# Decoder trunk on 8 cores: where RMSNorm squares are summed, the order of the first pass, the conv taps, and the last output tile

## Chip, cores, metric

The kernel runs on all 8 cores of one Trainium2 chip. Every core runs the same program on its own 2048 tokens (plus 144 tokens to the left and 16 meta tokens) and nothing is exchanged. The metric is the device time in microseconds (us) of the slowest core. Lower is better.

## What is computed

Four pre-norm residual layers over one stream h of 1024 channels, then a final RMSNorm. The mixers of layers 0 to 3 are attention, short convolution, pooling, attention; every layer ends with a SwiGLU FFN of width 2816.

```
def rms_norm(x, g):
    y = xf * lax.rsqrt(jnp.mean(xf * xf, axis=-1, keepdims=True) + RMS_EPS)
    return (y * g).astype(x.dtype)
# layer i
    a = rms_norm(h, norm_mix[i])
    h = h + mixer(a)          # attention: window 128, 16 meta keys, sinks, relative bias
    h = h + swiglu(rms_norm(h, norm_ffn[i]), w_gate, w_up, w_down)
# short_conv_mixer
    gate_b, gate_c, u = jnp.split(h @ w_in, 3, axis=-1)
    z = gate_c * u
    conv = sum(conv_w[t] * zp[:, t:t + L] for t in range(3))
    return (gate_b * conv) @ w_out
```

## The kernel before, in words

Channels lie on partitions, in KC = 8 chunks of 128; tokens are the columns. A core's 2208 columns are cut into three passes (`PASS`), and each pass into two tiles: 416 and 256 columns in pass 0, 384 and 384 in passes 1 and 2. The residual h stays in SBUF in f32. Weights stream through a ring of 6 slots of 512 KB (`load_unit`, on POOL's queue, converted to bf16 by the DMA). A group is 8 (or 7) matmuls of 128x128 weights against one tile, accumulated in one of eight PSUM banks (`group`).

Everything is written out as one static order. `_run(main, side, share)` walks the steps of `main`, which are mostly groups of matmuls with a cost each, and drops the steps of `side` between them in proportion. An engine executes its instructions in just that order; all engines wait only on semaphores that `Prog.op` derives from reads and writes. `merge` interleaves lists evenly.

**The norm.** `norm_steps` (line 394) has two ways to sum the squares of the 8 chunks. With `quads=False` (`square`) ACT writes each square in bf16 into one of 4 buffers `sq`, and PE sums over partitions and chunks with 8 matmuls against `onesb`, three steps behind. With `quads=True` (`square4`) ACT writes the squares in f32 into one of 3 buffers `sqf`, DVE adds them in two sets of four (3 adds each; the last writes bf16 to `sq`), and PE needs 2 matmuls. Then `root` takes ln and exp on ACT, and `scale` writes the 8 normed chunks on DVE.

**Attention.** `attn_in` projects queries, keys and values; ACT evicts q and k, DVE evicts v. `attn_core` works on items (a block of 64 queries and one of two pairs `pr` of key heads; pair 0 needs only query chunks 0 to 3). An item is: 4 score matmuls, two `exp` of 128x512 in place in PSUM on ACT, two multiplications with the bias table on DVE (to `Pt`), 8 matmuls for values and denominators, ln and exp of the denominator on ACT (`rden`), and one multiplication back on DVE. Items advance in half steps: item i's scores are issued, and a full step later its value matmuls.

**Stages.** `ffn(i)` runs the FFN of step i (i = 3 * layer + pass) with the mixer of step i+1 and the norm of step i+2 beside it. Where step i+1 is attention (i = 0, 1, 8, 9, 10) its items and the norm steps go beside the FFN's matmuls (`beside`), and these norms have `quads=False`. The lines at the end of `build` (1273 to 1294) are the first pass, before any FFN: tile 0's norm, then `first` (q, k, v of tile 0, with the exponentials of the bias tables on ACT, `tables`, at its end), `second` (tile 1's q, k, v, with the first items beside it), the queries of pass 1, and the output projection of pass 0's attention. PE has three banks for groups there (`MAIN3`).

**Convolution.** A step of `conv_in` (line 1033) runs three groups (B, C, u) for one chunk and tile. ACT copies u from PSUM to `sgt`; DVE forms z = C*u in `zt`, scales it by tap 0 into `cacc`, adds taps 1 and 2, and multiplies by B into `qt`. There is one `zt` and one `cacc`; banks 0 to 2 rotate for B, banks 3 to 5 for C and u. ACT carries the last two columns of z in `zcar`.

**The end.** In `ffn(11)` the last third of the down projection is done tile by tile (384, then 384). The final norm of the first tile runs beside the second tile's groups, that of the second tile after them; each normed quarter of a tile is stored as soon as it is there.

## Time and profile before

| | |
|---|---|
| time of 3 runs | 2802.86 to 2804.58 us, median 2804.21 |
| the profiled execution | 2803.19 us |
| its span, slowest core (5) | 2801.7 us (the others 2799.1 to 2801.1) |
| mean granted TensorE clock, by core | 0.988 to 0.991 |
| busy: PE, DVE, ACT | 97%, 57%, 40% of the span |
| chain that ended last | 90% PE, 4% DVE, 2% DMA, 2% ACT |

The span is the time from the first to the last instruction of one core; the execution's own time is 1.5 us above it. A busy PE is not PE at its peak: a matmul's end is modelled, and waits shorter than its pipeline don't show. PE's pace is better read from how many matmuls start in a stretch. The granted clock is given as a share of 2.4 GHz. Nearly all operations carry line 126, the line of `Prog.emit` that issues them, so groups are told apart by their tiles: `sb_abf<-sb_h` is a norm's scaling, `ps<-sb_sq,sb_onesb` the matmul that sums squares, `sb_h<-ps,sb_h` the addition to the residual.

### The profile page before, as it was taken

To read this page: it belongs to the slowest core of one execution; us is meant where nothing else is said; L and a number is where in the kernel's file an instruction comes from. 1 tells how busy PE (TensorE), PEld (TensorE's weight loads), DVE (VectorE), ACT (ScalarE), POOL (GpSimd) and SP (SyncE) were. 2 spreads that over 40 slices of the span, in tenths; PEclk is the share of its full clock that TensorE was granted. 3 is DMA by queue.
4 is the path that set the end of the run, shared out by engine and by line. 5 is a ranking of instruction groups with operands and counts; after the bars stand their busy time and mean duration, and the time that the engine had idled before them with its cause. 6 is when DMAs were issued, how large, how long until landed. Compare 5 with 4: busy or idle time off the path is not lost.

```text
span 2801.7 us, 53884 instructions; the slowest of 8 cores (2799.1 to 2801.7 us)
## 1 busy us (share of the span) xinstructions
PE 2711.6 (97%) x18214; PEld 1674.1 (60%) x18214; DVE 1584.9 (57%) x3182; ACT 1126.1 (40%) x2370; POOL 280.3 (10%) x532
## 2 busy tenths in 40 slices
...
GB/s 235 57 71 94 95 98 93 89 83 105 89 104 101 106 107 120 106 98 102 92 110 102 91 122 108 116 100 113 90 88 108 109 121 109 88 91 107 104 117 117
DMA packets 82974, 290.93 MB, mean 104 GB/s; under 512 B 9940, under 2 KB 11924, under 8 KB 81940
## 3 DMA queue, kind: packets, MB, share of 16 engines
...
q8 instruction: 155, 2.54, 0.4%
q14 instruction: 111, 0.91, 0.1%
...
## 4 chain that ended last, share of the span: by engine, by line
PE 90%; DVE 4%; DMA 2%; ACT 2%; issue 2%; DVEq 0%; ACTq 0%; SPq 0%; POOL 0%; POOLq 0%
PE ps L126 90%; DMA sb_h<-x 1%; ACT sb_sgt L126 1%; DVE sb_Pt L126 1%; DMA sb_ring<-attn_q 1%; DVE sb_scr L126 1%; DVE sb_abf L126 1%; DVE sb_qt L126 0%; DVE sb_abm L126 0%; ACT ps L126 0%; DVE sb_sgt L126 0%; DVE sb_sqf L126 0%; DVE sb_h L126 0%; DVE sb_gbf L126 0%; ACT sb_rden L126 0%
## 5 line engine op out<-in xcount | busy, mean ns | idle before, releaser
L126 PE MATMUL ps<-sb_abf,sb_ring 128*128 128x384 bf16 (+2 forms) x8608 | 1369.7, 318 | 15.6 <-DVE sb_qt L126 5.2
L126 PEld LDWEIGHTS ps<-sb_abf,sb_ring 128*128 128x128 bf16 x8608 | 834.9, 98 | 512.0 <-issue 53.7
L126 PE MATMUL ps<-sb_gbf,sb_ring 128*128 128x384 bf16 (+2 forms) x4352 | 699.0, 317 | 2.9 <-DVE sb_gbf L126 2.1
L126 PEld LDWEIGHTS ps<-sb_gbf,sb_ring 128*128 128x128 bf16 x4352 | 417.8, 98 | 253.3 <-issue 25.2
L126 ACT ACTIVATE sb_sgt<-ps 128x384 f32<-128x384 f32 (+2 forms) x528 | 247.5, 469 | 732.1 <-PE ps L126 642.0
L126 DVE TENSOR_TENSOR sb_gbf<-ps,sb_sgt 128x384 bf16<-128x384 f32 (+2 forms) x528 | 281.7, 533 | 457.8 <-PE ps L126 372.4
L126 DVE TENSOR_TENSOR sb_h<-ps,sb_h 128x384 f32<-128x384 f32 (+2 forms) x624 | 329.9, 533 | 241.5 <-PE ps L126 237.3
L126 PE MATMUL ps<-sb_abm,sb_ring 128*128 128x384 bf16 (+2 forms) x1952 | 316.9, 323 | 7.0 <-DVE sb_scr L126 2.9
L126 PEld LDWEIGHTS ps<-sb_abm,sb_ring 128*128 128x128 bf16 x1952 | 191.7, 99 | 127.4 <-issue 21.5
L126 POOL DMA_DIRECT2D sb_ring<-ffn_gu x264 | 140.7, 533 | 1225.1 <-PE ps L126 1224.5
L126 ACT ACTIVATE sb_sqf<-sb_h 128x384 f32<-128x384 f32 (+2 forms) x256 | 120.9, 498 | 276.2 <-DVE sb_sqf L126 196.9
L126 DVE TENSOR_TENSOR sb_sgt<-ps,sb_sgt 128x384 f32<-128x384 f32 (+2 forms) x206 | 106.6, 517 | 207.6 <-ACT sb_sgt L126 194.9
L126 PE MATMUL ps<-sb_qt,sb_ring 128*128 128x384 bf16 (+3 forms) x1136 | 180.2, 316 | 0.0
L126 ACT ACTIVATE ps<-ps 128x512 f32<-128x512 f32 (+2 forms) x270 | 141.9, 563 | 86.6 <-PE ps L126 86.6
L126 DVE TENSOR_TENSOR sb_Pt<-ps,sb_eb 128x512 bf16<-128x512 f32 (+3 forms) x272 | 167.0, 652 | 12.9 <-ACT ps L126 11.3
L126 PEld LDWEIGHTS ps<-sb_qt,sb_ring 128*128 128x128 bf16 x1136 | 110.6, 98 | 62.9
L126 POOL DMA_DIRECT2D sb_ring<-ffn_dn x144 | 76.0, 527 | 680.3 <-PE ps L126 680.0
L126 ACT ACTIVATE sb_sgt<-sb_sgt,sb_oneb 128x384 f32<-128x384 f32 (+2 forms) x206 | 120.2, 584 | 19.6 <-ACT sb_sgt L126 0.7
L126 DVE SCALAR_TENSOR_TENSOR sb_abf<-sb_h,sb_gam,sb_rstd 128x384 bf16<-128x384 f32 (+2 forms) x208 | 113.1, 584 | 19.0 <-ACT sb_rstd L126 18.9
L126 ACT ACTIVATE sb_sgt<-sb_sgt 128x384 f32<-128x384 f32 (+2 forms) x206 | 101.3, 492 | 20.0 <-ACT sb_sgt L126 1.5
L126 ACT ACTIVATE sb_sq<-sb_h 128x384 bf16<-128x384 f32 (+2 forms) x176 | 82.1, 495 | 52.8 <-PE ps L126 34.8
L126 PE MATMUL ps<-sb_sq,sb_onesb 128*128 128x384 bf16 (+2 forms) x242 | 68.3, 321 | 33.0 <-DVE sb_sq L126 30.3
...
## 6 DMA issues: line engine op xcount, KB each, us to landing
sb_ring<-ffn_gu POOLq DMA_DIRECT2D x264, 512.0 KB, 6.5
...
sb_ring<-ffn_dn POOLq DMA_DIRECT2D x48, 512.0 KB, 6.3
sb_ring<-conv_in POOLq DMA_DIRECT2D x36, 512.0 KB, 6.4
sb_ring<-attn_q POOLq DMA_DIRECT2D x24, 512.0 KB, 7.1
sb_ring<-attn_o POOLq DMA_DIRECT2D x24, 512.0 KB, 6.4
...
sb_ring<-conv_out POOLq DMA_DIRECT2D x12, 512.0 KB, 6.2
```

The lines of the kernel that those rows point to most:

```text
L126: ins = getattr(e, name)(*a_, **kw_)
```

## The change

- **Sum of squares.** `quads` becomes 0, 4 or 8. With 8, DVE adds all eight chunks (7 adds) and PE does 1 matmul. It is used for the norms that run beside attention (`mixer_prep` and `final` in `ffn(0)`, `ffn(1)`, `ffn(8)`, `ffn(9)`, `ffn(10)`; 8 matmuls per tile before) and for the FFN norm beside the convolution of pass 0 in layer 1 (also 8 before). Pass 0's first norm goes from 4 (6 adds, 2 matmuls) to 0 (8 matmuls).
- **First pass.** Tile 0's q chunks 4 to 7 move behind its k and v (`more`), the items of pair 0 on tile 0's blocks come first, and all 23 items become one list that is cut over four stretches. PSUM: three banks for scores and one for outputs, for two and two. The loads that follow x's first tile on SP's queue wait until that tile has landed.
- **Convolution.** Tap 0 is applied by ACT into `sgt`, z has two buffers, and taps 1 and 2 with the product by B are issued one step later, behind the next step's z.
- **End.** Pass 2's last third of the down projection and its final norm use tiles of 384, 256 and 128 columns.

```diff
-OUT_TILES = tuple(n for _, n in LAST_TILES0) + tuple(n for p in PASS[1:] for _, n in p["tiles"])
+END_TILES = ((0, 384), (384, 256), (640, 128))
+OUT_TILES = tuple(n for t in (LAST_TILES0, PASS[1]["tiles"], END_TILES) for _, n in t)
...
-    zt = scr[:, 0:420]
-    cacc = scr[:, 420:836]
+    zts = [scr[:, 420 * i:420 * i + 420] for i in range(2)]
...
-    small += sload(attb[:], ab_d.rearrange("l p c -> p l c"), "s1", ("attb",))
+    P.op("sp", _I.dma_start(out=attb[:], in_=ab_d.rearrange("l p c -> p l c")), reads=[B("h", k, 0) for k in range(KC)],
+         writes=[B("attb")], dma="s1")
+    small.append(B("attb"))
...
-            if 0 <= j < KC and j % 4:
+            if 0 <= j < KC and j % quads:
                 f = st["f"][j]
-                acc = st["f"][j - 1] if j % 4 == 1 else st["acc"]
-                if j % 4 == 3:
+                acc = st["f"][j - 1] if j % quads == 1 else st["acc"]
+                if j % quads == quads - 1:
                     si = ctr["sq"] % NSQ
                     ctr["sq"] += 1
-                    st["sq"][j // 4] = si
+                    st["sq"][int(j == 7)] = si
                     out, key = sq[:, si, 0:n], B("sq", si)
                 else:
                     out, key = sqf[:, f, 0:n], B("sqf", f)
                     st["acc"] = f
                 P.op("dve", _I.tensor_tensor(out=out, in0=sqf[:, acc, 0:n], in1=sqf[:, f, 0:n], op=ALU.add),
                      reads=[B("sqf", acc), B("sqf", f)], writes=[key])
-            if k in (7, 11):
-                total(st["sq"][k // 8], k == 7, k == 11)
+            if (k == 7 and quads == 4) or k == 11:
+                total(st["sq"][k // 8], k == 7 or quads == 8, k == 11)
...
-        tiles = out_tiles(l, p)
+        tiles = END_TILES if last else out_tiles(l, p)
...
                 part = [(8 * t[1], lambda c=c, t=t: qstep(c, t)) for c in range(KC)]
+                if ti == 0:
+                    part, more = part[0:4], part[4:]
...
+                parts.append(part)
                 if ti == 0:
                     part.append((0, tables))
-                parts.append(part)
+                    parts.append(more)
...
-            items.append(("m", 0, 0, NMETA))
-            items += [(-3, pr, 16, 16) for pr in range(2)]
+
+            for pr in range(2):
+                items += [("m", 0, 0, NMETA)][0:pr] + [(-3, pr, 16, 16)] + [(jb, pr, _hbcol(p, jb), 64) for jb in range(-2, 4)]
         j0, j1 = PASS[p]["hb"]
-        if p == 0 and l > 0:
-            j0 = 0
+        if p == 0:
+            j0 = 0 if l > 0 else 4
...
-            P.op("act", _I.copy(out=sgt[:, si, 0:n], in_=ps[bU][:, 0:n]), reads=[psb[bU]], writes=[B("sgt", si)])
-            P.op("act", _I.copy(out=zt[:, 0:2], in_=zcar[:, c, :]), reads=[B("zcar", c)], writes=[B("zt2")])
-            P.op("dve", _I.tensor_tensor(out=zt[:, 2:2 + n], in0=ps[bC][:, 0:n], in1=sgt[:, si, 0:n], op=ALU.mult),
-                 reads=[psb[bC], B("sgt", si)], writes=[B("zt")])
-            P.op("act", _I.copy(out=zcar[:, c, :], in_=zt[:, n:n + 2]), reads=[B("zt")], writes=[B("zcar", c)])
-            P.op("dve", _I.tensor_scalar_mul(out=cacc[:, 0:n], in0=zt[:, 0:n], scalar1=cw[:, c:c + 1]),
-                 reads=[B("zt"), B("zt2"), B("cw")], writes=[B("cacc")])
-            for tap in (1, 2):
-                P.op("dve", _I.scalar_tensor_tensor(out=cacc[:, 0:n], in0=zt[:, tap:tap + n],
-                                                    scalar=cw[:, tap * KC + c:tap * KC + c + 1], in1=cacc[:, 0:n],
-                                                    op0=ALU.mult, op1=ALU.add),
-                     reads=[B("zt"), B("zt2"), B("cw"), B("cacc")], writes=[B("cacc")])
-            P.op("dve", _I.tensor_tensor(out=qt[:, c, t[0]:t[0] + n], in0=ps[bB][:, 0:n], in1=cacc[:, 0:n], op=ALU.mult),
-                 reads=[psb[bB], B("cacc")], writes=tk("qt", c, t[0], t[0] + n))
+            z, zk, z2 = zts[ti], B("zt", ti), B("z2", ti)
+            S = sgt[:, si, 0:n]
+            P.op("act", _I.copy(out=S, in_=ps[bU][:, 0:n]), reads=[psb[bU]], writes=[B("sgt", si)])
+            P.op("act", _I.copy(out=z[:, 0:2], in_=zcar[:, c, :]), reads=[B("zcar", c)], writes=[z2])
+            P.op("dve", _I.tensor_tensor(out=z[:, 2:2 + n], in0=ps[bC][:, 0:n], in1=S, op=ALU.mult),
+                 reads=[psb[bC], B("sgt", si)], writes=[zk])
+            P.op("act", _I.copy(out=zcar[:, c, :], in_=z[:, n:n + 2]), reads=[zk], writes=[B("zcar", c)])
+            P.op("act", _I.activation(out=S, in_=z[:, 0:n], func=AF.Identity, scale=cw[:, c:c + 1]),
+                 reads=[zk, z2, B("cw")], writes=[B("sgt", si)])
+
+            def taps():
+                for tap in (1, 2):
+                    P.op("dve", _I.scalar_tensor_tensor(out=S, in0=z[:, tap:tap + n], scalar=cw[:, tap * KC + c:tap * KC + c + 1], in1=S,
+                                                        op0=ALU.mult, op1=ALU.add),
+                         reads=[zk, z2, B("cw"), B("sgt", si)], writes=[B("sgt", si)])
+                P.op("dve", _I.tensor_tensor(out=qt[:, c, t[0]:t[0] + n], in0=ps[bB][:, 0:n], in1=S, op=ALU.mult),
+                     reads=[psb[bB], B("sgt", si)], writes=tk("qt", c, t[0], t[0] + n))
+            if late[0]:
+                late[0]()
+            late[0] = taps
+            if c == KC - 1 and ti == len(PASS[p]["tiles"]) - 1:
+                late[0] = None
+                taps()
...
-        prep = mixer_prep(i + 2, not has_core(i + 1))
+        prep = mixer_prep(i + 2, 8 if has_core(i + 1) else 4)
         if l == NLAYER - 1 and p > 0:
-            prep = final(p - 1, ((0, 0), (0, 1))[p - 1], not has_core(i + 1))
+            prep = final(p - 1, ((0, 0), (0, 1))[p - 1], 8 if has_core(i + 1) else 4)
...
-                (s0, e0), (s1, e1) = norm_ffn(*lp(i + 1), quads=lp(i + 2)[0] != 1)
+                (s0, e0), (s1, e1) = norm_ffn(*lp(i + 1), quads=8 if lp(i + 2)[0] == 1 else 4)
...
-            end = final(2, (0, 1), quads=False)
+            end = final(2, (0, 1, 2), quads=0)
             _run(dn[2][0:KC])
-            _run(dn[2][KC:], end[0])
-            for step in end[1]:
+            _run(dn[2][KC:2 * KC], end[0][0:NSTAT + 1])
+            _run(dn[2][2 * KC:], merge(end[0][NSTAT + 1:], end[1]))
+            for step in end[2]:
...
-    prep, prep1 = mixer_prep(0), mixer_prep(1)
+    prep, prep1 = mixer_prep(0, 0), mixer_prep(1)
     for step in prep[0]:
         step()
     load_late((2, 3), tk("abf", 7, 0, 32))
-    first, second = attn_in(0, 0, 0)
+    first, more, second = attn_in(0, 0, 0)
     queries, keys = attn_in(0, 0, 1)
     _run(first, prep[2] + prep[1], 0.9)
+    main_banks[0], s_banks[0], o_banks[0], n_banks[0] = MAIN3, (3, 4, 5), (6,), (7, 7)
+    core = attn_core(0, 0, attn_items(0, 0))
+    _run(more + second, merge(core[0:17], prep1[0]))
     load_late((4, 5), tk("gbf", 7, 0, 32))
-    items = attn_items(0, 0)
-    main_banks[0], s_banks[0], o_banks[0], n_banks[0] = MAIN3, (3, 4), (5, 6), (7, 7)
-    core0, core1 = attn_core(0, 0, items[0:15]), attn_core(0, 0, items[15:])
-    _run(second, core0[0:10] + prep1[0])
     P.alias([B("xl"), B("abl"), B("ebm")], tall("qt"))
-    _run(queries[0:KC + 1], core0[10:16] + prep1[1])
-    _run(queries[KC + 1:], core0[16:])
+    _run(queries[0:KC + 1], merge(core[17:28], prep1[1]))
+    _run(queries[KC + 1:], core[28:39])
     out0 = mixer_out(0)
-    _run(out0[0:KC], core1)
+    _run(out0[0:KC], core[39:])
```

How it moves instructions, at three places. On PE in the first pass, around tile 1's q groups (`sb_abf` 128x256), before:

```order
L126 MATMUL ps<-sb_Pt,sb_ones 64x256 x4
L126 MATMUL ps<-sb_abf,sb_ring 128x256 x24
L126 MATMUL ps<-sb_sq,sb_onesb 128x384
L126 MATMUL ps<-sb_abf,sb_ring 128x256 x8
L126 MATMUL ps<-sb_sq,sb_onesb 128x384
L126 MATMUL ps<-sb_abf,sb_ring 128x256 x16
L126 MATMUL ps<-sb_ring,sb_abf 128x256 x16
L126 MATMUL ps<-sb_abm,sb_ring 128x384 x8
```

and in the change:

```order
L126 MATMUL ps<-sb_sq,sb_onesb 128x384
L126 MATMUL ps<-sb_abf,sb_ring 128x256 x8
L126 MATMUL ps<-sb_gbf,sb_kt 128x256 x4
L126 MATMUL ps<-sb_abf,sb_ring 128x256 x8
L126 MATMUL ps<-sb_Pt,sb_va 64x256 x2
L126 MATMUL ps<-sb_Pt,sb_vbo 64x256 x2
L126 MATMUL ps<-sb_Pt,sb_ones 64x256 x4
L126 MATMUL ps<-sb_abf,sb_ring 128x256 x8
L126 MATMUL ps<-sb_gbf,sb_kt 128x256 x4
```

Before, six of tile 1's groups have no attention between them; now an item's scores or values stand between nearly every two groups. On DVE at the start of pass 0's convolution in layer 1 (a step of 416 columns, then one of 256; `sb_abf` is the FFN norm beside it), before:

```order
L126 TENSOR_TENSOR sb_scr<-ps,sb_sgt 128x416
L126 TENSOR_SCALAR sb_scr<-sb_scr,sb_cw 128x416
L126 SCALAR_TENSOR_TENSOR sb_scr<-sb_scr,sb_cw 128x416 x2
L126 TENSOR_TENSOR sb_qt<-ps,sb_scr 128x416
L126 SCALAR_TENSOR_TENSOR sb_abf<-sb_h,sb_gam,sb_rstd 128x384 x2
L126 TENSOR_TENSOR sb_scr<-ps,sb_sgt 128x256
```

and in the change:

```order
L126 TENSOR_TENSOR sb_scr<-ps,sb_sgt 128x416
L126 SCALAR_TENSOR_TENSOR sb_abf<-sb_h,sb_gam,sb_rstd 128x384 x2
L126 TENSOR_TENSOR sb_scr<-ps,sb_sgt 128x256
L126 SCALAR_TENSOR_TENSOR sb_sgt<-sb_scr,sb_cw,sb_sgt 128x416 x2
L126 TENSOR_TENSOR sb_qt<-ps,sb_sgt 128x416
```

The z of the second step now stands ahead of the first step's taps, and the TENSOR_SCALAR is gone. On DVE at the very end, the last tiles' residual additions and scalings, before:

```order
L126 TENSOR_TENSOR sb_h<-ps,sb_h 128x384 x13
L126 SCALAR_TENSOR_TENSOR sb_abm<-sb_h,sb_gam,sb_rstd 128x384
L126 TENSOR_TENSOR sb_h<-ps,sb_h 128x384
L126 SCALAR_TENSOR_TENSOR sb_abm<-sb_h,sb_gam,sb_rstd 128x384 x3
L126 TENSOR_TENSOR sb_h<-ps,sb_h 128x384
L126 SCALAR_TENSOR_TENSOR sb_abm<-sb_h,sb_gam,sb_rstd 128x384 x2
L126 TENSOR_TENSOR sb_h<-ps,sb_h 128x384
L126 SCALAR_TENSOR_TENSOR sb_abm<-sb_h,sb_gam,sb_rstd 128x384 x2
L126 SCALAR_TENSOR_TENSOR sb_qt<-sb_h,sb_gam,sb_rstd 128x384 x8
```

and in the change:

```order
L126 TENSOR_TENSOR sb_h<-ps,sb_h 128x384 x8
L126 TENSOR_TENSOR sb_h<-ps,sb_h 128x256 x8
L126 TENSOR_TENSOR sb_h<-ps,sb_h 128x128 x8
L126 SCALAR_TENSOR_TENSOR sb_abm<-sb_h,sb_gam,sb_rstd 128x384 x5
L126 SCALAR_TENSOR_TENSOR sb_qt<-sb_h,sb_gam,sb_rstd 128x256
...
L126 SCALAR_TENSOR_TENSOR sb_qt<-sb_h,sb_gam,sb_rstd 128x256 x2
L126 SCALAR_TENSOR_TENSOR sb_qt<-sb_h,sb_gam,sb_rstd 128x128 x8
```

All scalings, those of the 384 tile too, now stand behind the last addition: the 128-column groups have a negative cost in `_run` (7 * 128 - 1300), so no side step is placed between them.

## Rows read from the trace of the kernel before

**Rows 1.** Page, head and part 1: span, busy time and share by engine.

```profile
span 2801.7 us, 53884 instructions; the slowest of 8 cores (2799.1 to 2801.7 us)
...
PE 2711.6 (97%) x18214; PEld 1674.1 (60%) x18214; DVE 1584.9 (57%) x3182; ACT 1126.1 (40%) x2370; POOL 280.3 (10%) x532
```

**Rows 2.** Stretches: PE, PEld, DVE, ACT, POOL busy (count), PEclk, DMA share, GB/s.

```profile
1240.00:1280.00 40.00, 40.00 (x248) 24.10 (x247) 15.05 (x28) 3.88 (x8) 3.70 (x7) 1.00 0.60 100
```

**Rows 3.** The same view, stretches of the first pass.

```profile
53.24:83.64 30.40, 21.05 (x153) 13.29 (x150) 15.83 (x42) 19.99 (x46) 2.64 (x5) 0.78 0.74 158
83.64:113.36 29.72, 21.97 (x113) 9.72 (x111) 18.46 (x37) 14.18 (x30) 0.53 (x1) 0.83 0.22 35
113.36:140.81 27.45, 23.33 (x149) 10.56 (x149) 16.15 (x34) 17.04 (x36) 1.58 (x3) 0.75 0.31 54
140.81:170.41 29.60, 22.89 (x163) 10.55 (x161) 17.69 (x32) 14.80 (x33) 0.53 (x1) 0.94 0.13 23
```

**Rows 4.** PE's waits from 53.24 to 170.41: us in total, times, longest.

```profile
PE ps L126 <- DVE sb_Pt L126: 14.5, 22, 2.0
PE ps L126 <- DVE sb_sq L126: 7.1, 3, 3.4
```

**Rows 5.** Timeline of POOL and ACT, start of the first pass: start us, us, instruction.

```profile
15.10 1.58 POOL L126 DMA_DIRECT2D sb_ring<-attn_q  x3 [12.88 <-DMA sb_h<-x]
49.78 3.60 ACT L126 ACTIVATE sb_eb<-sb_eb 128x4096 f32<-128x4096 f32 x1
58.71 0.41 ACT L126 ACTIVATE sb_qt<-sb_sinkst 1x256 f32<-1x256 f32 x1
```

**Rows 6.** Issues up to 62 us: KB each, median us to landing.

```profile
sb_ring<-attn_v POOLq DMA_DIRECT2D x1, 512.0 KB, 30.5
```

**Rows 7.** Timeline of PE in `ffn(1)` beside attention, two sums of squares.

```profile
642.53 0.49 PE L126 MATMUL ps<-sb_sq,sb_onesb 128*128 128x384 bf16 x2
642.86 1.46 PE L126 MATMUL ps<-sb_qt,sb_ring 128*128 128x384 bf16 x8
```

**Rows 8.** Groups by form, whole span: busy us, mean ns | idle before, releasers.

```profile
L126 DVE TENSOR_TENSOR sb_sqf<-sb_sqf 128x384 f32<-128x384 f32 x80 | 44.1, 552 | 21.2 <-ACT sb_sqf L126 18.7 <-DVE sb_sqf L126 2.2 <-ACT sb_gbf L126 0.2
...
L126 DVE TENSOR_TENSOR sb_sqf<-sb_sqf 128x256 f32<-128x256 f32 x28 | 11.8, 421 | 14.6 <-ACT sb_sqf L126 13.7 <-DVE sb_sqf L126 0.9
```

**Rows 9.** Stretches as in rows 2: FFN beside attention; conv of pass 0; after it.

```profile
2240.00:2280.00 40.00, 39.12 (x371) 30.39 (x371) 29.14 (x66) 32.18 (x76) 4.23 (x8) 1.00 0.69 113
...
650.33:715.63 65.30, 57.15 (x394) 37.84 (x392) 48.71 (x97) 16.52 (x58) 6.94 (x13) 0.99 0.68 111
715.63:721.10 5.47, 5.47 (x18) 2.54 (x19) 0.02 (x1) 1.77 (x2) 0.00 (x0) 0.50 0.27 50
```

**Rows 10.** PE's waits from 650 to 721 us.

```profile
PE ps L126 <- DVE sb_qt L126: 5.2, 1, 5.2
PE ps L126 <- DVE sb_scr L126: 2.9, 6, 0.8
```

**Rows 11.** Groups by form: the tap that leaves DVE.

```profile
L126 DVE TENSOR_SCALAR sb_scr<-sb_scr,sb_cw 128x384 f32<-128x384 f32 x32 | 13.4, 420 | 5.6 <-DVE sb_scr L126 5.6
```

**Rows 12.** The end: stretch (as rows 2), then DVE's timeline; last, 256-column scalings elsewhere.

```profile
2776.70:2801.70 25.00, 12.61 (x74) 6.98 (x72) 14.00 (x25) 9.00 (x17) 0.00 (x0) 0.83 0.33 127
...
2790.26 0.55 DVE L126 TENSOR_TENSOR sb_h<-ps,sb_h 128x384 f32<-128x384 f32 x1
2793.68 5.10 DVE L126 SCALAR_TENSOR_TENSOR sb_qt<-sb_h,sb_gam,sb_rstd 128x384 f32<-128x384 f32 x8 [1.61 <-ACT sb_rstd L126]
```

**Rows 13.** Small forms: PE's timeline near 45 us; DVE's scaling of 256 and of 144 columns.

```profile
44.88 0.66 PE L126 MATMUL ps<-sb_qt,sb_ring 128*128 128x144 bf16 x8
45.38 1.57 PE L126 MATMUL ps<-sb_abf,sb_ring 128*128 128x416 bf16 x8
...
52.25 0.88 DVE L126 SCALAR_TENSOR_TENSOR sb_abf<-sb_h,sb_gam,sb_rstd 128x256 bf16<-128x256 f32 x2
...
L126 DVE SCALAR_TENSOR_TENSOR sb_qt<-sb_qt,sb_gam,sb_rstd 128x144 bf16<-128x144 f32 x8 | 2.9, 368 | 3.6 <-ACT sb_rstd L126 2.9
```

More of the change, by code:

```diff
@@ L459, in scale @@
             ri = st["ri"]
-            P.op("dve", _I.scalar_tensor_tensor(out=dst(k), in0=hsrc(k), scalar=g[:, k:k + 1], in1=rstd[:, ri, 0:n],
+            P.op(eng, _I.scalar_tensor_tensor(out=dst(k), in0=hsrc(k), scalar=g[:, k:k + 1], in1=rstd[:, ri, 0:n],
                                                 op0=ALU.mult, op1=ALU.mult),
@@ L486, in q_of, with norm_mix @@
         return (gbf, "gbf") if (l, p) == (0, 0) else (qt, "qt")
-    def norm_mix(l, p, quads=True):
+    def norm_mix(l, p, quads=4):
         parts = []
@@ L587, in ffn_gu, with ffn_dn @@
         return steps
-    def ffn_dn(l, p, g, tile_major=False):
+    def ffn_dn(l, p, g, last=False):
         steps = []
@@ L601, in ffn_dn @@
         order = [(m, ti) for m4 in (0, 4) for ti in range(len(tiles)) for m in range(m4, m4 + 4)]
-        if tile_major:
+        if last:
             order.sort(key=lambda x: x[1])
@@ L1038, in prelude @@
             if p == 0:
-                claim("scr", [B("zt"), B("zt2"), B("cacc")])
+                claim("scr", [B("zt", i) for i in range(2)] + [B("z2", i) for i in range(2)])
         def step(c, ti, t):
@@ L1142, in build, with final @@
     out_sems = []
-    def final(p, regions, quads=True):
+    def final(p, regions, quads=4):
         parts = []
-        for t, r in zip(out_tiles(NLAYER - 1, p), regions):
+        for t, r in zip(END_TILES if p == NPASS - 1 else out_tiles(NLAYER - 1, p), regions):
             src, keys = h_tile(p, t)
             n = t[1]
-            name = ("abm", "qt")[r]
+            name = ("abm", "qt", "qt")[r]
             quarter = [B("yf", r, i) for i in range(KC // 2)]
-            y = (abm_raw, qt_raw)[r][:, 0:2 * KC * n].bitcast(F32)
+            y0 = 2 * KC * 256 if r == 2 else 0
+            y = (abm_raw, qt_raw, qt_raw)[r][:, y0:y0 + 2 * KC * n].bitcast(F32)
             def begin(name=name, quarter=quarter):
@@ L1162, in store @@
                      reads=[quarter[i]], dma=sem)
-                if i == KC // 2 - 1:
+                if i == KC // 2 - 1 and p < NPASS - 1:
                     P.alias(quarter, tall(name))
             steps = norm_steps(src, keys, n, gcol("fin", 0), lambda k, y=y, n=n: y[:, k * n:(k + 1) * n],
-                               lambda k, quarter=quarter: [quarter[k // 2]], quads)[0]
+                               lambda k, quarter=quarter: [quarter[k // 2]], quads,
+                               "pool" if POOL_SCALE and p == NPASS - 1 and r == 0 else "dve")[0]
             ends = [[steps[NSTAT + 2 * i], steps[NSTAT + 1 + 2 * i], lambda i=i, store=store: store(i)] for i in range(KC // 2)]
@@ L1176, in lp, with mixer_prep @@
         return i // NPASS, i % NPASS
-    def mixer_prep(i, quads=True):
+    def mixer_prep(i, quads=4):
         if i >= N:
```

11 lines of the change are left out of this document (6 added, 5 removed).

## The prediction

> **What bounds the kernel now.** I read the page's head and busy shares first, then stretches of 40 us, then PE's waits, then timelines where a stretch falls short. PE is busy 97% of the span, DVE 57%, ACT 40% [rows 1]. A typical FFN stretch starts 248 matmuls of 384 columns in 40 us, one per 0.161 us at full clock [rows 2]: that is PE's pace, 0.42 ns per column. So from the first FFN to the last tile the time is the sum of PE's columns, and work on DVE or ACT there costs nothing while it is on time. Three places fall short. (1) The first pass: in 117 us from 53.24 to 170.41 PE's clock is 0.75 to 0.94, and PE waits 14.5 us for `Pt` and 7.1 us for sums of squares [rows 3, 4]. (2) The convolution of pass 0: PE waits 2.9 us in six gaps for z and 5.2 us in one at the end, and the clock stands at 0.50 for the next 5.5 us [rows 9, 10]. (3) The last 25 us, of which PE works 12.6 [rows 12].
>
> **Sums of squares.** In the steady part the change takes 7 of 8 `onesb` matmuls from each of 12 tiles: two in each of the steps 0, 1, 8, 9 and 10, and two in the FFN norm before the convolution. That is 56 matmuls of 384 columns, 7 of 416 and 21 of 256. Two of them take 0.33 us [rows 7], the pace of any other. By columns 56 x 0.161 + 7 x 0.175 + 21 x 0.108 = 12.5 us. PE is the bound there, so this is taken whole: **-12.5 us**.
>
> In exchange DVE gets 7 adds per tile, 84 in all, at 0.55 us (384), 0.42 (256) and about 0.58 (416) [rows 8]: 56 x 0.55 + 21 x 0.42 + 7 x 0.58 = 43.7 us. In the fullest stretch beside attention DVE is busy 29.1 and ACT 32.2 of 40 us [rows 9]. There are 12 steps in 2801.7 us, some 230 us each, so 14 adds (8 us) bring DVE's load up by some 4%. The adds go in one per side step. A square must now wait until the add two places back has read its buffer; that add sits behind at most a few DVE instructions, as in the norms that already sum this way, where DVE's adds wait for ACT 18.7 us over 80 adds rather than the other way for long [rows 8]. The softmax chain behind it on ACT is what PE would notice. I take **+1.5 us**, near nothing, because PE shows about a microsecond lost even in the fullest stretch (39.12 of 40) [rows 9]; the ends are 0 and +10 (a quarter of the adds open).
>
> **First pass.** From 53.24 to 170.41 at full pace PE would need: 128 matmuls of 384 (20.6 us), 96 or so of 256 (10.4), 64 of 416 (11.2), and 20 items of 12 matmuls of 256 (26), together 68 us of 117. ACT is busy 66.0 us and DVE 68.1 us in the same stretch (sums over rows 3). [rows 3] No engine is full, so what limits is the chain of an item (scores, exp, weigh, values) with too little between its links in some places and no item at all in others. By stage, needed over taken: 13.6 of 30.4 (0.45), 15.5 of 29.7 (0.52), 22 of 27.5 (0.80), 22 of 29.6 (0.74). The thin ones are those where q groups stand alone while the dense ones wait on `Pt` [rows 3, 4]. The change spreads the items at 5 to 6 per eight groups. If every stage reaches the 0.77 of the two dense ones, 68 us take 88; 32 matmuls of tile 0's q that move in add 5.6 / 0.77 = 7 us, and they leave a stretch that waits for ring loads, so their going gives nothing there. That is 95 for 117: -22. Against it: the table exponentials hold ACT from 49.8 to 59.1 [rows 5] and can't be spread, and with three banks PE gets past them by three groups only; +4. For it: k and v are the third and fourth ring loads, not the fifth and sixth; v lands at 17.2 + 30.5 = 47.7 us now [rows 6] and I expect the order to give 2 to 4 us, of which I count 1. The load of x's first tile has the DMA engines to itself and the next ring loads wait for it until 15.1 us [rows 5]; with bf16 squares and no add behind the last one, -2; the bias table then is issued some 11 us later, which eats 1. In sum **-20 us**.
>
> The ends: everything in time, PE at its own need of 74 us in the stretch, gives -43; the late table load or one output bank (a value matmul waits until the item before is multiplied back) could take all of it and 5 us more, +5. I take the middle because the estimate rests on two stages of this very trace.
>
> Of the 49 us lost in the stretch the clock is a part: 0.22 x 30.4 + 0.17 x 29.7 + 0.25 x 27.5 + 0.06 x 29.6 = 20.4 us of full pace not granted [rows 3], which is 41 us at 1.2 instead of 2.4 GHz. So an order that keeps the clock up and changes no gap at all would still give up to -20. The Trainium skill puts the price of the clock in the same way (TensorE: Matmul & The Clock Gate, section "HAM oscillation — how this bites in real kernels"): the extra wall time of a throttled stretch is its length times one minus the clock ratio. By that page the whole gain of the first pass could be clock, with the gaps as they are, where my sum by stages lays it to closed gaps; the trace agrees on the size with its 20.4.
>
> **Convolution.** Behind a z stood the taps of the step before and two scalings; now z is first, and 0.42 us per step goes to ACT [rows 11], which is busy only 16.5 of 65 us [rows 9]. DVE needs 48.7 of 65.3 us there now; it loses 6 and gains the second tile's adds. The six gaps (2.9 us) close. The last one stays: the FFN's first group needs the bank of the last B, which is read after two steps' taps; copy 0.4, z 0.4, taps and product 1.9 and 1.5, so about 4.4 for 5.2. The half clock behind it stays. **-3.5 us**; ends -8 (clock kept) and 0.
>
> **The end.** The second tile starts at 2776.7; its last addition ends at 2790.8, the last scaling at 2798.8, the span at 2801.7 [rows 12], 25.0 us after it. Changed: 56 matmuls of 256 (6.0), 8 sums (1.3) and 56 of 128 columns. 144-column matmuls start every 0.063 us [rows 13], so these take at most 3.5. The last addition is done 11.2 us after the start, 2.9 earlier. But all 24 scalings now come after it: 5.1 (384) [rows 12], 8 x 0.44 = 3.5 (256), 8 x 0.32 = 2.6 (128, below the 0.37 of 144 columns) [rows 13]. They end at 22.4, where they end now at 22.1, and the last store follows with 2.9: **0 us**. Ends: -3 (PE's sums of the small tiles hidden and cheaper scalings) and +2.
>
> The last store gets three times smaller. The Trainium skill (DMA: Bandwidth & Descriptors, "Anatomy of one DMA — SWDGE (gpsimd) path") puts a transfer at about 2.0 us plus its bytes over 436 GB/s. By that estimate 393 KB cost 2.9 us, which is what the trace shows behind the last scaling, and 131 KB cost 2.3: the end would be -0.6, not 0.
>
> **Sum.** 2803.2 - 12.5 + 1.5 - 20 - 3.5 + 0 = 2768.7, against the profiled execution; the median of the runs is 1 us above it. I say **2769**.
>
> **Rivals.**
> - *The first pass hardly moves.* The chain of an item, not the spacing, sets the pace: one output bank now, the same two exps and two weighs. For it: PE's longest single waits are on `Pt` [rows 4], and the dense stages are no better than 0.80. Against: two stages at 0.45 to 0.52. The first pass gives -20 to 0; 2779 to 2789, and with costly adds up to 2798.
> - *It closes whole.* With the gaps the half clock goes too; -38 instead of -20, about 2750. For it: each engine needs under 60% of the time. Against: the tables, the loads.
> - *The adds lie open (slower).* Each add delays a square, the square the exp behind it on ACT, the exp a score or value matmul at which PE stands. Price: all 43.7 us. Then 2768.7 + 42 = 2811. It decides from about 35 us on, four adds of five. Against: the fullest stretch has DVE idle 11 of 40 us, and each add has a whole side step to pass in.
> - *The clock stays down.* Evenly spread short waits could keep PE at 1.2 GHz through the first pass, where now it is granted 0.75 to 0.94: at 0.6 the 74 us take 123, so the stretch gains nothing, 2791.
>
> **How the numbers follow.** About 0.2% (5.6 us) is what a measurement of this kernel tells from no change. Forecast (2757 to 2779): 0.52. First pass hardly moves or clock down (2779 to 2798): 0.26. Closes whole (2740 to 2757): 0.14. Within 5.6 us of before: 0.04. Slower by more, by open adds: 0.04. Hence faster 0.92. The range 2748 to 2792 leaves out the tails of both neighbours, about 2 in 10.
>
> **What would show it.** Right: 64 fewer matmuls on `onesb`, the small last tile's included; the stretches beside attention start the same groups 12 us sooner in sum, with PE still at 39 to 40 of 40; the first FFN begins some 20 us earlier; in the convolution no PE wait on `sb_scr`, one of 4 to 5 us at its end, and half a clock after it; at the end 24 scalings in a row on DVE. Wrong: ACT waiting for `sb_sqf` by tens of us with PE waiting on `Pt` in the stretches from 200 to 600 and 2150 to 2500 us; the first pass's clock at 0.8 or lower with as many waits on `Pt`; the last 25 us longer or shorter by more than 3.

## The result and the profile after

The changed kernel takes 2772.55 and 2774.99 us; the ratio to the kernel before is 0.9893, with a 95% interval of 0.9869 to 0.9917: 30 us less (23 to 37). I had said 2769, range 2748 to 2792. Some executions run on the cores of a die at a lower granted clock and take longer (two of this kernel's four, 2837.6 and 3140.9 us); they are left out of what follows, as are such cores in *The first pass alone* and *Eight chunks in the other norms too*. The execution profiled below took 2772.55 us; its slowest core is core 0 (before: core 5). It has PE at 97%, DVE at 57% and ACT at 41% of the span, as in [rows 1]:

```profile
span 2771.0 us, 53987 instructions; the slowest of 8 cores (2767.8 to 2771.0 us)
...
PE 2689.8 (97%) x18206; PEld 1665.3 (60%) x18206; DVE 1590.7 (57%) x3222; ACT 1148.8 (41%) x2428; POOL 280.2 (10%) x532
```

To see where 30 us went I cut both traces at the same places in the program. The rows are stretches (PE, PEld, DVE, ACT, POOL busy, PEclk, DMA share, GB/s). First the kernel before: up to the first FFN; from it to the convolution of layer 1, pass 0; the middle, from some 44 us behind that convolution to the first FFN with layer 3's attention beside it; from there to the last FFN (attention late).

```profile
0.00:194.90 194.90, 136.84 (x867) 72.80 (x868) 111.19 (x233) 101.32 (x219) 11.42 (x25) 0.89 0.56 123
194.90:650.33 455.43, 454.83 (x3198) 271.81 (x3196) 273.59 (x527) 263.68 (x546) 43.64 (x82) 1.00 0.55 92
...
759.89:1946.52 1186.63, 1183.16 (x7622) 745.04 (x7620) 675.01 (x1382) 317.56 (x653) 131.89 (x250) 1.00 0.63 106
1946.52:2535.46 588.94, 581.51 (x4330) 368.72 (x4330) 358.74 (x730) 350.35 (x750) 59.50 (x111) 1.00 0.59 101
```

Then the same of the changed kernel, with its convolution (that of before is in [rows 9]) and the 44 us behind it:

```profile
0.00:174.44 174.44, 125.54 (x878) 68.92 (x879) 103.64 (x221) 99.32 (x219) 11.42 (x25) 0.92 0.63 137
174.44:625.81 451.37, 449.85 (x3164) 268.33 (x3162) 288.11 (x562) 263.89 (x546) 43.63 (x82) 1.00 0.57 93
625.81:689.93 64.12, 56.32 (x386) 36.85 (x385) 45.34 (x88) 23.60 (x75) 6.87 (x13) 0.98 0.69 111
689.93:733.86 43.93, 43.93 (x257) 25.83 (x257) 8.37 (x15) 9.56 (x19) 3.70 (x7) 0.95 0.55 93
733.86:1920.50 1186.64, 1183.17 (x7622) 744.96 (x7621) 658.04 (x1350) 334.01 (x685) 131.92 (x250) 1.00 0.65 105
1920.50:2505.02 584.52, 575.95 (x4288) 364.48 (x4288) 375.44 (x772) 350.28 (x750) 59.49 (x111) 1.00 0.61 101
```

The gain by stage: first pass 20.5, next stage 4.1, convolution 1.2 (65.30 to 64.12), the 44 us behind it 0.3, the middle nothing (1186.63 and 1186.64), attention late 4.4, and from there to the end 0.3 (266.24 to 265.98). That is 30.7, the difference of the spans is 30.7. Between the first FFN and the last tile the same code takes the same time to 0.1 us on every core, but for a stretch of low clock behind the convolution (43.3 to 44.3 us there), so these lengths tell apart what the interval of the runs, some 7 us each way, can't. The start and the end don't repeat so well. The first FFN begins between 192.4 and 195.1 us on the eight cores before (median 194.6), and between 171.6 and 174.4 now (median 173.1); from the last stage's start to the end of the span it is 266.0 to 266.3 us before and 266.0 to 266.6 now, so the 0.3 us there are nothing. Where single cores differ so, I compare the medians of all eight.

**The start** did not gain. The changed kernel, timelines of PE, ACT and SP's queue (start us, us, instruction, idle before it and what ended it):

```profile
18.77 7.13 PE L126 MATMUL ps<-sb_abf,sb_ring 128*128 128x416 bf16 x16 [2.37 <-DVE sb_abf L126]
36.76 0.28 PE L126 MATMUL ps<-sb_sq,sb_onesb 128*128 128x144 bf16 x1 [10.86 <-DVE sb_sq L126]
...
29.21 0.61 ACT L126 ACTIVATE sb_gbf<-ps,sb_attb 128x416 bf16<-128x416 f32 x1 [11.42 <-DMA sb_qt<-bias_mm]
34.63 0.75 ACT L126 ACTIVATE sb_sqf<-sb_qt 128x144 f32<-128x144 f32 x3 [4.81 <-DMA sb_qt<-x]
...
14.63 0.39 SPq L126 DMA_DIRECT2D sb_attb<-attn_b  x1
...
18.18 0.59 SPq L126 DMA_DIRECT2D sb_qt<-x  x1
```

The held bias table stands ahead of everything else in SP's queue, so the 144 columns of x on the left are issued at 18.18 instead of 8.08 us and land only when ACT starts on them at 34.63; their first sum stands in PE's order, and PE waits 10.9 us. In and behind that wait its clock is granted at half for about 14 us: 0.81 from 19.2 to 35.0 and 0.83 from 35.0 to 58.0, which is 0.38 x 15.8 + 0.34 x 23.0 us at 1.2 GHz (what of it lies inside the wait costs nothing). The v groups that ended at 53.24 end at 56.74 (medians 53.3 and 56.5).

**The rest of the first pass** more than made up for it. Stretches as in [rows 3], the last one up to the first FFN, then PE's waits from 56.74 to 149.70 as in [rows 4]:

```profile
56.74:86.80 30.06, 24.50 (x196) 13.98 (x193) 21.73 (x50) 26.22 (x57) 1.06 (x2) 0.89 0.46 127
86.80:130.70 43.90, 36.14 (x294) 18.63 (x290) 32.29 (x71) 32.07 (x75) 3.93 (x8) 1.00 0.57 101
130.70:149.70 19.00, 17.04 (x125) 8.57 (x124) 12.09 (x23) 10.23 (x23) 0.30 (x1) 1.00 0.20 38
149.70:174.44 24.74, 20.76 (x143) 14.78 (x142) 17.39 (x39) 9.68 (x21) 2.63 (x5) 0.86 0.69 107
...
PE ps L126 <- DVE sb_gbf L126: 7.0, 8, 2.8
PE ps L126 <- DVE sb_Pt L126: 5.9, 4, 3.5
```

The 117.2 us of [rows 3] have become 93.0 with 5.6 us more of work in them. The waits for `Pt` fell from 14.5 us in 22 places to 5.9 in 4. New are 7.0 us in 8 places for the multiplication back (`gbf`), which frees the one output bank; they were 0.9 us in one place before. The clock is granted whole from 86.8 to 149.7 on this core (core 2 has 0.97 there), and at 0.86 in the stretch behind, which takes 24.7 us for 24.5.

**The convolution of pass 0.** PE's waits in it; they answer to [rows 10]:

```profile
PE ps L126 <- DVE sb_qt L126: 7.6, 8, 4.9
PE ps L126 <- DVE sb_scr L126: 0.2, 1, 0.2
```

The waits for z are gone, 2.9 us to 0.2, and seven new ones, 2.7 us in all, stand beside the long one, which is 4.9. What they are for shows in the timelines of PE and DVE at one of them:

```profile
640.08 2.62 PE L126 MATMUL ps<-sb_abm,sb_ring 128*128 128x416 bf16 x14 [0.43 <-DVE sb_qt L126]
...
637.84 0.59 DVE L126 TENSOR_TENSOR sb_scr<-ps,sb_sgt 128x416 f32<-128x416 f32 x1 [0.98 <-ACT sb_scr L126]
638.35 1.06 DVE L126 SCALAR_TENSOR_TENSOR sb_sgt<-sb_scr,sb_cw,sb_sgt 128x256 f32<-128x256 f32 x2
639.51 0.42 DVE L126 TENSOR_TENSOR sb_qt<-ps,sb_sgt 128x256 bf16<-128x256 f32 x1
```

DVE makes z of this step (416 columns), then the taps and the product of the step before (256). PE's next group is the B of the step after next, and B has three banks in turn: it needs the one that this product reads. A step of 256 columns leaves it 2.6 us after the last U, and ACT's copy, z, two taps and a product take about that (0.51 + 0.59 + 1.06 + 0.42), so PE waits at the end of each of these.

**The end** came out as worked. DVE's last two rows and SP's last:

```profile
2757.54 3.12 DVE L126 SCALAR_TENSOR_TENSOR sb_abm<-sb_h,sb_gam,sb_rstd 128x384 f32<-128x384 f32 x5 [0.16 <-DVE sb_h L126]
...
2764.93 4.00 DVE L126 SCALAR_TENSOR_TENSOR sb_qt<-sb_h,sb_gam,sb_rstd 128x256 f32<-128x256 f32 x10
...
2766.06 3.27 SPq L126 DMA_DIRECT2D out<-sb_qt  x5
```

All 24 scalings follow the last addition without a gap, 2757.54 to 2768.93 us, 11.4 us; the span ends 2.1 us later, not 2.9. Counted from the second tile's first matmul, the last scaling ends at 22.7 us on all cores, where it ended at 22.0 before, and the span ends 2.1 to 2.7 us behind it, where it was 2.7 to 3.0: the later scalings and the shorter tail cancel.

### The profile page after: what moved, and what is told of

The parts are those of the page before. It is cut to its first block, busy times and chain, and to the rows that moved or that the text cites. A ratio compares the mean times of both kernels' runs of the same rounds, so it can differ in the third digit from the quotient of the medians.

```text
span 2771.0 us, 53987 instructions; the slowest of 8 cores (2767.8 to 2771.0 us)
## 1 busy us (share of the span) xinstructions
PE 2689.8 (97%) x18206; PEld 1665.3 (60%) x18206; DVE 1590.7 (57%) x3222; ACT 1148.8 (41%) x2428; POOL 280.2 (10%) x532
## 4 chain that ended last, share of the span: by engine, by line
PE 89%; DVE 4%; ACT 3%; issue 2%; DMA 1%; SPq 0%; DVEq 0%; ACTq 0%
PE ps L126 89%; ACT sb_sgt L126 2%; DVE sb_Pt L126 1%; DVE sb_qt L126 1%; DVE sb_sgt L126 1%; DMA sb_qt<-x 1%; DVE sb_scr L126 1%; ACT ps L126 0%; DMA sb_h<-x 0%; DVE sb_gbf L126 0%; DVE sb_abm L126 0%; DVE sb_sqf L126 0%; DVE sb_abf L126 0%; DVE sb_h L126 0%; ACT sb_sqf L126 0%
## 5 line engine op out<-in xcount | busy, mean ns | idle before, releaser
L126 PE MATMUL ps<-sb_abf,sb_ring 128*128 128x384 bf16 (+2 forms) x8608 | 1366.2, 318 | 11.4 <-DVE sb_qt L126 4.9
L126 DVE TENSOR_TENSOR sb_h<-ps,sb_h 128x384 f32<-128x384 f32 (+3 forms) x632 | 330.8, 527 | 229.5 <-PE ps L126 224.2
L126 PE MATMUL ps<-sb_abm,sb_ring 128*128 128x384 bf16 (+2 forms) x1952 | 308.7, 318 | 5.6 <-DVE sb_qt L126 2.7
L126 ACT ACTIVATE sb_sqf<-sb_h 128x384 f32<-128x384 f32 (+2 forms) x336 | 160.0, 496 | 292.6 <-DVE sb_sqf L126 209.0
L126 DVE TENSOR_TENSOR sb_sqf<-sb_sqf 128x384 f32<-128x384 f32 (+3 forms) x196 | 102.0, 520 | 46.1 <-ACT sb_sqf L126 41.9
L126 ACT ACTIVATE sb_sgt<-sb_sgt,sb_oneb 128x384 f32<-128x384 f32 (+2 forms) x206 | 120.2, 584 | 19.6 <-ACT sb_sgt L126 0.8
```

The costliest lines, as they stand in the source:

```text
L126: ins = getattr(e, name)(*a_, **kw_)
```

## The experiments

All run on all cores beside the kernel before; "alone" is on the kernel before, the others on the changed one.

**The sums alone.** The edit, with its three callers giving 8 beside attention and convolution:

```diff
-            if 0 <= j < KC and j % 4:
+            if 0 <= j < KC and j % quads:
...
-            if k in (7, 11):
-                total(st["sq"][k // 8], k == 7, k == 11)
+            if (k == 7 and quads == 4) or k == 11:
+                total(st["sq"][k // 8], k == 7 or quads == 8, k == 11)
```

> The kernel before with the sums over eight chunks alone. Theory (from the two traces): the 84 ones-matmuls gone are 12.2 us of PE's columns, and the added DVE adds give about 2 us of it back in short waits near attention, so about 2794 us (-10). Rival 1: the adds cost PE nothing and the missing gain lies in another part, 2791.5 (-12.3). Rival 2: the adds lie open, 2800 or more.

2797.1 us median, ratio 0.9979 (0.9967 to 0.9990), about -6. Three stages on core 5, as above: before the convolution, the convolution, attention late.

```profile
196.20:647.22 451.02, 449.81 (x3163) 268.37 (x3161) 288.04 (x561) 263.82 (x546) 43.64 (x82) 1.00 0.55 93
647.22:713.63 66.41, 56.33 (x387) 36.96 (x385) 52.26 (x104) 16.77 (x59) 7.09 (x13) 0.97 0.64 108
...
1943.60:2528.58 584.98, 576.15 (x4287) 364.39 (x4287) 376.10 (x772) 350.47 (x750) 59.52 (x111) 1.00 0.59 101
```

The two stages beside attention give 4.4 and 4.0 us. 77 of the 84 ones-matmuls lie there (49 of 384 columns, 7 of 416, 21 of 256), 11.4 us at 0.42 ns a column, so the adds cost 3.0 us of them. In the convolution it is 1.1 us longer with 1.1 us fewer columns: seven adds cost 2.2 us where DVE has 52.3 of 66.4 us to do. So the sums alone give some 7 us by stages, and beside the late taps, where the convolution gains its 1.2 us, some 8. The theory's -10 is not reached in either.

**The taps alone.**

```diff
-            P.op("dve", _I.tensor_scalar_mul(out=cacc[:, 0:n], in0=zt[:, 0:n], scalar1=cw[:, c:c + 1]),
+            P.op("act", _I.activation(out=S, in_=z[:, 0:n], func=AF.Identity, scale=cw[:, c:c + 1]),
...
+            if late[0]:
+                late[0]()
+            late[0] = taps
```

> The kernel before with the late taps alone. Theory: the six waits for z (2.9 us) are replaced by as many short waits for the B bank, whose product now comes a step later, so the convolution of pass 0 keeps its length: 2803 to 2804.5 us (0 to -1), with PE waiting some 2.5 us in short gaps on the product. Rival, my prediction: -3.5, 2800.5; then it is the second tile's adds that refill the gaps in the changed kernel.

Ratio 0.9996 (0.9985 to 1.0008). The convolution takes 63.87 us for 65.30; PE's waits in it:

```profile
PE ps L126 <- DVE sb_qt L126: 6.3, 4, 5.0
PE ps L126 <- ACT sb_sq L126: 0.2, 1, 0.2
```

Alone the late taps give 1.4 us: three short waits for the bank, 1.3 us, for six of 2.9. With the second tile's adds on DVE there are seven. So both halves of the question hold: the waits moved to the bank, and the adds made more of them. The run's ratio can't show 1.4 us; the stage does, at 63.8 to 63.9 us on all eight cores.

**The first pass alone.** The order of the items, the banks, bf16 squares and the hold, as in the change.

> The kernel before with the new first pass alone (bf16 squares, held bias table, early k and v, even items, three score banks and one output bank). Theory: all of the 20.5 us by which the first FFN starts earlier reaches the end: about 2783.5 us (-20.5), first FFN at 174 us. Rival: the pass gains only together with other parts, or the later passes give some of it back (x tiles 2 to 5 load later): 2786 to 2793.

There is no ratio for this run; cores 4 to 7 span 2778.7 to 2781.1 us, some 20 below before. On core 6:

```profile
0.00:171.83 171.83, 124.18 (x878) 68.31 (x879) 103.36 (x221) 99.48 (x219) 11.47 (x25) 0.94 0.64 139
171.83:627.28 455.45, 454.84 (x3198) 271.86 (x3196) 273.75 (x527) 264.01 (x546) 43.84 (x82) 1.00 0.55 92
```

The stage behind it keeps its 455.4 us: nothing is given back, the theory holds.

**The split last tile alone.**

```diff
+END_TILES = ((0, 384), (384, 256), (640, 128))
...
-            _run(dn[2][KC:], end[0])
+            _run(dn[2][KC:2 * KC], end[0][0:NSTAT + 1])
+            _run(dn[2][2 * KC:], merge(end[0][NSTAT + 1:], end[1]))
```

> The kernel before with the split last tile alone. Theory: the later start of the scalings cancels the earlier last addition, 2803.5 us (0 to -0.5). Rival: the smaller last store and the cheaper scalings show, -2 to -3, and in the whole change something else takes them back.

Ratio 1.0006 (0.9994 to 1.0018): no change, as expected.

**No hold.** The bias table and what stands behind it in SP's queue are issued at once:

```diff
-    P.op("sp", _I.dma_start(out=attb[:], in_=ab_d.rearrange("l p c -> p l c")), reads=[B("h", k, 0) for k in range(KC)],
-         writes=[B("attb")], dma="s1")
+    small += sload(attb[:], ab_d.rearrange("l p c -> p l c"), "s1", ("attb",))
```

> The changed kernel, its bias table, x_left and x tile 1 issued at once again (no hold behind x tile 0). Theory: the hold is a loss. In the changed trace the 16 first matmuls end at 25.9 us and PE then stands 10.9 us for the sums of x_left, which lands at 34.6 because it was issued at 18.2; ACT's drain waits for the bias table until 29.2. Without it x_left lands some 8 to 10 us sooner, the first FFN starts 4 to 7 us earlier (168 to 170 us), the time is 2766 to 2769. Rival (my prediction): x tile 0 alone on the DMA engines is a gain; without the hold the first q group starts 1 to 2 us later and the end too, 2774 to 2776.

2767.3 us, ratio 0.9865 (0.9844 to 0.9886). Timeline of PE:

```profile
18.84 7.22 PE L126 MATMUL ps<-sb_abf,sb_ring 128*128 128x416 bf16 x16 [2.37 <-DVE sb_abf L126]
26.05 0.28 PE L126 MATMUL ps<-sb_sq,sb_onesb 128*128 128x144 bf16 x1
30.33 2.93 PE L126 MATMUL ps<-sb_abf,sb_ring 128*128 128x416 bf16 x8 [4.00 <-DMA sb_ring<-attn_q]
```

The first q group starts at 18.84 here against 18.77 us on core 0 of the changed kernel, but that core is the latest of its eight. On core 4, with the hold and without:

```profile
18.01 2.19 PE L126 MATMUL ps<-sb_abf,sb_ring 128*128 128x416 bf16 x4 [2.37 <-DVE sb_abf L126]
...
18.91 1.07 PE L126 MATMUL ps<-sb_abf,sb_ring 128*128 128x416 bf16 x2 [2.37 <-DVE sb_abf L126]
```

By medians the first q group starts at 18.1 with the hold (17.8 to 18.8) and at 18.9 without (18.3 to 19.2): alone on the DMA engines x's first tile does land some 0.8 us sooner, as the rival has it. But without the hold the sum of x_left is there when PE comes to it, and 4.0 us of waiting for weights stand where 10.9 stood. The first FFN starts at 166.1 to 169.4 us, median 166.7 for 173.1: in sum the hold cost 6.4 us.

**The hold moved to x tile 1.** As above, with `reads=` of x tile 0 at `x_load(1, "x2")`.

> The changed kernel, the hold moved from the bias table to x tile 1 (1 MB), so that the small tables and x_left go at once and the large loads behind x tile 0. Theory: takes the gain of both, first FFN at 166 to 170 us, 2764 to 2768, not slower than without any hold. Rival: the second x tile, whose sums stand in PE's order at 48 to 52 us, lands later and gives part of it back: same as with the hold, 2772.

2768.3 and 2767.8 us, ratio 0.9867 (0.9846 to 0.9889); first FFN at 166.5 to 169.8, median 167.5. No better than no hold: holding the large loads has no use either, and the first q group starts at 18.9 as without any, so the 0.8 us above are given by holding what stands ahead of x tile 1.

**Two score and two output banks.**

```diff
-    main_banks[0], s_banks[0], o_banks[0], n_banks[0] = MAIN3, (3, 4, 5), (6,), (7, 7)
+    main_banks[0], s_banks[0], o_banks[0], n_banks[0] = MAIN3, (3, 4), (5, 6), (7, 7)
```

> The changed kernel with two score banks and two output banks in the first pass, as before, in place of three and one. Theory A: the even spacing of the items made the gain, and the first FFN starts within 3 us of the changed kernel's 174.4 us (2771 to 2776). Theory B: the third score bank made it, since an item's scores can be issued while the two exps of the item before still hold theirs: the first FFN starts at 180 to 190 us, 2778 to 2788.

2778.4 us, ratio 0.9905 (0.9890 to 0.9921); first FFN at 175.8 to 180.7 us, median 178.9. PE's longest group of waits in the pass:

```profile
PE ps L126 <- DVE sb_Pt L126: 9.8, 13, 3.7
```

The time is in theory B's range, the start of the first FFN between the two. The waits for `gbf`, 7.0 us with one output bank, are gone, and those for `Pt` are 9.8 in 13 places for 5.9 in 4. So some 6 of the 21 us are what a third score bank gives beyond what the second output bank did; the rest is left to the spacing and order of the items, which no run changed by themselves. The single output bank, in which I saw the danger, does make PE wait and is still the better trade.

**C, U, B.** A convolution step issues its groups in another order:

```diff
-            banks = []
-            for part in range(3):
+            banks = {}
+            for part in (1, 2, 0):
```

> The changed kernel with the three groups of a convolution step in the order C, U, B. Theory: the short waits in the convolution of pass 0 are for the B bank, which the late product of three steps before still holds when B is the first group of a step; as the last group it is asked for two groups later, so all seven or so (0.6 us each, some 3 us) go, and the last one falls from 5.1 to about 3.5 us: -3 to -5 from 625.8 to 733.9 us, 2768 to 2770. Rival: the wait is DVE's pace (it needs as long as PE in this stretch), and the gaps only move to another bank: 2772 to 2774.

2770.2 us, ratio 0.9873 (0.9856 to 0.9891). The stage, and PE's waits in it:

```profile
629.25:688.59 59.34, 55.22 (x387) 37.46 (x386) 45.34 (x88) 23.74 (x75) 6.86 (x13) 1.00 0.65 112
...
PE ps L126 <- DVE sb_qt L126: 3.9, 1, 3.9
PE ps L126 <- DVE sb_scr L126: 0.2, 1, 0.2
```

The seven short waits are gone with DVE as loaded as before (45.34 and 45.34 us): they were for the bank, not DVE's pace. The stage gives 4.8 us, and the other convolutions in the middle another 2.5 (1184.1 for 1186.6). The run shows less, since on its slowest core the first FFN happened to start at 177.9 and late attention took 586.3 us, as on three of the eight cores (584.8 on the others).

**C, U, B, and the FFN's banks turned by three.** Three more `nxt("main", main_banks[0])` at the end of this convolution, so that the FFN's first group doesn't ask for the last B's bank.

> The changed kernel with the convolution in the order C, U, B, and the rotation of FFN's banks moved on by three after the convolution of pass 0, so that the FFN's first groups take the banks of the last C and U and reach the last B's bank fourth, not first. Theory: the remaining wait of 3.9 us goes, 59.3 us become 55.5 to 56, and with it perhaps the 6.8 us of half clock behind it (another 2 to 3): 2762 to 2766. Rival: the wait is for something else (the FFN's input), and stays: 2768 to 2770 as with C, U, B alone.

2765.3 us, ratio 0.9862 (0.9845 to 0.9879).

```profile
627.16:683.00 55.84, 55.24 (x388) 37.47 (x386) 42.41 (x83) 23.14 (x74) 5.81 (x11) 1.00 0.65 114
683.00:724.59 41.59, 41.59 (x256) 25.04 (x257) 11.30 (x21) 10.18 (x21) 4.75 (x9) 1.00 0.69 116
724.59:1912.49 1187.90, 1183.69 (x7623) 744.83 (x7620) 658.47 (x1350) 334.28 (x685) 131.90 (x250) 1.00 0.64 105
...
PE ps L126 <- DVE sb_qt L126: 3.2, 4, 2.1
```

The long wait goes (3.5 us), and the half clock behind it (42.9 to 44.3 us become 41.6, at 1.00). But the turn shifts the banks of later passes too, and the middle takes 1187.9 us (up to 1189.3 on other cores), 3.8 to 5.2 more than with C, U, B alone. The last row shows where: in the middle PE waits four times, 3.2 us, for a product (`qt`), each time at the start of the FFN behind a later convolution; with C, U, B alone it waits there for none. The banks should be turned back after use, which was not tried.

**Each add of the eight-chunk sums twice.**

```diff
+                for _ in range(2 if quads == 8 else 1):
```

> The changed kernel with each add of the sums over eight chunks made twice, 588 - 504 = 84 more DVE adds of about 0.52 us (43.7 us of DVE); the repeated add counts a chunk twice, so the sums themselves are changed. Theory: the first copy cost PE 2.6 us beside attention and some 2 in the convolution of pass 0, since DVE has slack nearly everywhere; the second costs as much or a little more: +4 to +9, 2777 to 2782, most of it where DVE is fullest (the convolution of pass 0 and the stretches beside attention). Rival 1: the 2.6 us are something else than DVE's load (the ACT square that waits for the add two places back), then the second copy delays squares more and costs +10 to +25. Rival 2: no cost, 2773.

(84 is 12 tiles by 7; the difference written there is a slip.) 2790.6 us median, ratio 0.9949 (0.9931 to 0.9966), about 16 above the changed kernel. By stage +7.8, +2.8 to +4.3 and +3.4. Rival 1 is right in size, and at this place in kind. PE's timeline in the first of these, at the FFN norm ahead of the convolution:

```profile
634.81 0.48 PE L126 MATMUL ps<-sb_sq,sb_onesb 128*128 128x384 bf16 x1 [5.00 <-DVE sb_sq L126]
```

This one late sum is 5.0 of the 7.8 us, and PE being busy 2.2 us longer with the same matmuls, with half clock behind the wait, is nearly all the rest. So at least a third of the run's price isn't paid by the microsecond of DVE but where a chain of eight squares and adds no longer ends before PE comes to its one ones-matmul; of the +3.4 late, 2 us are short waits of PE.

**Eight chunks in the other norms too.** `quads` 8 for the remaining 4.

> The changed kernel with the sums over eight chunks in the remaining norms that add on VectorE as well (ten tiles of the FFN phases without attention: 20 ones-matmuls fewer, 7 of 384 columns or so out of 8, and as many more adds). Theory: DVE has slack there, the columns are gained whole: -3.0, 2769.5 to 2770. Rival: adds in a loaded stretch cost as much as they give, 2772 to 2773.

Ratio 0.9884 (0.9860 to 0.9908). By stages on cores 0 to 3 the middle takes 1185.0 us for 1186.6 and the stage before the convolution 451.2 for 451.4, but late attention 585.1 for 584.5: 1.3 of the 3.0 us.

**All that helped.**

> All that helped, in one kernel: no hold, C, U, B, the bank rotation, eight chunks' sums everywhere. Theory: the parts lie in different stretches and add up: -6.3 (hold) -7.4 (C, U, B) -4 to -6 (rotation) -3 (sums) from 2772.6: 2750 to 2753. Rival: they share the cover of DVE, and a third is lost: 2756 to 2760.

2756.6 and 2759.3 us, ratio 0.9836 (0.9812 to 0.9859): 46 us below the kernel before, some 16 below the change. From the first FFN to the end of the last matmul it takes 2577.3 to 2578.3 us, some 10 less than the changed kernel (2587.0 to 2587.6), and the first FFN starts at 163.9 to 170.4. The middle's loss by the bank turn is in it. Within about 1 us the parts add up by stage; the core whose first FFN comes last (170.4) and that loss put the run's time at the rival's number, not the rival's reason, a shared cover of DVE.

## Why the prediction was right, and where it was not

- **The total**, -34.5 forecast and -30.7 measured between the spans. The sums gave some 8 for 11 and the late taps 1.4 for 3.5; the first pass, the end and the clock make up the rest.
- **Sums**, -12.5 + 1.5, measured some -8. The 84 ones-matmuls are gone as counted. The adds cost 3.0 us beside attention for my 1.5, and more in the convolution. The mechanism named, a chain of squares that ends too late for PE, is the one that the doubled adds show; the cover left is thin at the last add of the norm.
- **First pass**, -20, measured -20.5: right as a sum, partly by luck: the start lost 3.5 us where I had it gain, the stretch gained 24.2 where I had 18, and 0.2 was lost behind. The stretch was worked out at 117 - 22 + 4 = 99 us and took 93.0. The working had an error too: the needs by stage add up to 73 us where the total says 68, because the third stage (57 matmuls of 384 columns and 92 of 256) needs 19 and not 22, so its pace is 0.70 and not 0.80, and the two dense stages give 0.72, not 0.77. With that pace the sum would have been some 15 for my 22. The changed stretch runs at 74 of 93.0, 0.80, better than any rate I could read before. PE has 77.7 us busy for 89.2 with 5.6 us more of work, so 17.2 us are clock, and its idle time fell from 27.9 to 15.3 us, 12.6: -17.2 - 12.6 + 5.6 = -24.2. The Trainium skill (TensorE: Matmul & The Clock Gate, "HAM oscillation — how this bites in real kernels") prices a throttled stretch at its length times one minus the clock ratio; by that the loss fell from 20.4 to 0.11 x 30.1 = 3.3 us, 17.1, and the trace agrees. I had asked whether the clock is the whole gain or the gaps: it is both, about 17 to 13. The table exponentials, priced at +4, can't be told apart in it: all of PE's waits there end on DVE.
- **The start**, -2 for the hold and bf16 squares, +1 for the late table. This step failed, though its first link held: by medians the first q group starts at 18.1 for 19.6, 0.8 of it by the hold. The v groups end 3.5 us later, not 2 earlier. I asked who else needs the DMA engines, not what stands behind the held issue in SP's queue: x_left, whose sum stands in PE's order in the middle of the q groups. Without the hold they end 3.5 us earlier than before (49.8 for 53.3), and the pass gives 28 (all medians).
- **Convolution**, -3.5, measured about -1.2 with the 1.1 us of columns in it; the taps alone gave 1.4, and the seven adds beside them cost 1.3 (1.4 + 1.1 - 1.2), so nothing of its own is left. With the sums this is the step that made the total 4 us too good. "Behind a z stood the taps of the step before" is right, and the six gaps did close; but a product that comes a step later holds its bank a step longer, and PE comes back for that bank after three. C, U, B shows it.
- **The end**, 0, measured 0 within the spread of the cores. 24 scalings in 11.4 us for my 11.2; the last store lands 2.1 to 2.7 us after the last scaling, not 2.9, and the scalings end 0.7 later than before, where I had 0.3. The Trainium skill (DMA: Bandwidth & Descriptors, "Anatomy of one DMA — SWDGE (gpsimd) path") gave an estimate of 2.3 for a store of that size on GpSimd's queue. These stores go from SP's; the trace's 2.1 to 2.7 agree with it better than my 2.9.
- **Rivals.** The open adds did not come, and doubled they cost a third of their length, not all. The clock stayed up where the items are, 0.89 to 1.00 for 0.75 to 0.94, and fell to 0.81 to 0.86 ahead of and behind them. That one output bank makes PE wait was right, 7.0 us of it; that this would hold the pass back against two and two was wrong by its sign.
